# The output projection taken token tile by token tile, and the first up-projection block in token form, in a hybrid decoder layer on one core

## The reference

```python
x = x + (gate_ret * y_ret + gate_moba * y_moba) @ w_out[l]
h = rms_norm(x, ffn_norm[l])
u = causal_depthwise_conv(h @ w_up[l], conv_w[l], conv_b[l])
u_gate, u_val = jnp.split(u, 2, axis=-1)
x = x + (jax.nn.silu(u_gate) * u_val) @ w_down[l]
```

## Time and profile before

| | |
|---|---|
| time, median of 3 runs | 488.93 us (488.80 to 488.98) |
| span of the profiled execution | 486.9 us |
| outside the span (median less span) | 2.0 us |
| PE busy | 475.4 us (98%) |
| PEld busy | 439.7 us (90%) |
| DVE busy | 296.1 us (61%) |
| ACT busy | 249.0 us (51%) |
| POOL busy | 17.1 us (4%) |
| HBM traffic | 177 GB/s over the span |

### The profile page before, as it was taken

How to read it: one execution, slowest core, us unless ns; L and a number is a source line. 1 busy time by engine, 2 the same in 40 slices (tenths; PEclk the granted TensorE clock), 3 DMA queues, 4 the chain that set the end, 5 groups by cost and what they waited for, 6 DMA issues and landing times.

```text
span 486.9 us, 7961 instructions
## 1 busy us (share of the span) xinstructions
PE 475.4 (98%) x3183; PEld 439.7 (90%) x3183; DVE 296.1 (61%) x354; ACT 249.0 (51%) x354; POOL 17.1 (4%) x26
## 2 busy tenths in 40 slices
PE   6999999999999999999999989999999999999997
PEld 4789999888888999999999868999999999988885
DVE  3854884574665546355337856488888777886312
ACT  3735332345884739333444625566666666673310
POOL 1000000311110001000000010000000000000000
PEclk9999999999999999999999997999999999999999
DMA  8996255144455524843453562144545555539002
GB/s 314 355 346 256 104 199 224 48 139 166 168 172 187 219 114 142 333 168 133 165 195 131 194 228 105 69 172 172 176 181 187 194 194 192 189 132 363 3 1 86
DMA packets 13400, 86.65 MB, mean 178 GB/s; under 512 B 1472, under 2 KB 1856, under 8 KB 3648
## 3 DMA queue, kind: packets, MB, share of 16 engines
q1 hardware_dynamic: 12096, 82.84, 45.7%
q10 hardware_dynamic: 864, 1.88, 1.1%
q0 software_dynamic: 416, 1.57, 0.9%
HBM read 85.24 MB, written 1.05 MB: 177 GB/s over the span
## 4 chain that ended last, share of the span: by engine, by line
PE 95%; DMA 1%; DVE 1%; ACT 1%; issue 0%; POOL 0%; POOLq 0%; SPq 0%
PE bank L333 18%; PE bank L334 18%; PE bank L335 18%; PE bank L293 7%; PE bank L295 7%; PE bank L294 7%; PE bank L526 4%; PE bank L523 4%; PE bank L524 4%; PE bank L350 2%; DMA xs<-x_dram 1%; PE bank L429 1%; PE bank L411 1%; PE bank L430 0%; PE bank L410 0%
## 5 line engine op out<-in xcount | busy, mean ns | idle before, releaser
L775 DVE TENSOR_TENSOR w_lo<-w_raw,w_hi 128x2048 fp32r<-128x2048 f32 x75 | 170.3, 2288 | 79.5 <-ACT w_hi L548 79.4
L333 PE MATMUL bank<-h_hi,w_hi 128*128 128x256 f32 x608 | 173.5, 285 | 0.7 <-DVE h_lo L980 0.7
L334 PE MATMUL bank<-h_lo,w_hi 128*128 128x256 f32 x608 | 172.7, 284 | 0.0
L335 PE MATMUL bank<-h_hi,w_lo 128*128 128x256 f32 x608 | 172.7, 284 | 0.0
L548 ACT ACTIVATE w_hi<-w_raw 128x2048 fp32r<-128x2048 f32 x75 | 141.6, 1915 | 33.4 <-PE bank L526 16.9
L333 PEld LDWEIGHTS bank<-h_hi,w_hi 128*128 128x128 f32 x608 | 117.5, 193 | 1.2 <-issue 1.1
L334 PEld LDWEIGHTS bank<-h_lo,w_hi 128*128 128x128 f32 x608 | 117.5, 193 | 0.1
L335 PEld LDWEIGHTS bank<-h_hi,w_lo 128*128 128x128 f32 x608 | 117.4, 193 | 0.0
L293 PE MATMUL bank<-w_hi,h_hi 128*128 128x512 f32 x160 | 63.1, 395 | 0.3 <-DVE w_lo L780 0.2
L295 PE MATMUL bank<-w_hi,h_lo 128*128 128x512 f32 x160 | 62.4, 390 | 0.0
L294 PE MATMUL bank<-w_lo,h_hi 128*128 128x512 f32 x160 | 62.3, 389 | 0.0
(11 more groups left out here) (112 smaller groups left out, 435.4 us busy)
## 6 DMA issues: line engine op xcount, KB each, us to landing
w_raw<-weights_dram SPq DMA_DIRECT2D x76, 1024.0 KB, 4.9
xs<-x_dram SPq DMA_DIRECT2D x2, 512.0 KB, 5.2
w_raw<-weights_dram SPq DMA_DIRECT2D x2, 512.0 KB, 8.3
xs<-x_dram POOLq DMA_DIRECT2D x1, 1024.0 KB, 7.9
out_dram<-ys SPq DMA_DIRECT2D x4, 256.0 KB, 2.0
area<-decay_dram ACTq DMA_DIRECT2D x1, 768.0 KB, 4.1
area<-gain_rows_dram ACTq DMA_DIRECT2D x1, 512.0 KB, 7.0
area<-gain_rows_dram POOLq DMA_DIRECT2D x1, 512.0 KB, 10.7
```

Source lines behind the costliest of these rows:

```text
L333: mm(o, s_hi, r_hi[:, k, :], start=(k == 0 and m % 2 == 0), stop=False)
L334: mm(o, s_hi, r_lo[:, k, :], start=False, stop=False)
L335: ins = mm(o, s_lo, r_hi[:, k, :], start=False, stop=(k == KT - 1 and m % 2 == 1))
L775: tt(w_lo[r][:, :], raw[r][:, :], w_hi[r][:, :].bitcast(f32), ALU.subtract).then_inc(lo_ready, 1)
```

## The change

1. **The output projection goes by token tiles.** For t = 0 all four halves 40 to 43 are taken (12 matmuls each), then for t = 1. Residual, squares, inverse root and normalisation follow for each tile by itself. The transposes of tile 0 stand ahead of the last quarter of tile 1.
2. **The block UP0 (halves 44, 45) is computed in token form**, tile by tile, with the same helper. The transposes of tile 1's normalised activations stand in the middle of tile 0's second half.
3. **It is transposed back.** ACT copies the 128 x 512 result of each token tile to `y_tok` (`up_tok_read`), PE transposes it (4 transposes for a tile: `up_transposes`), the first tile's ahead of the next up block (half 46), the second tile's between halves 46 and 47. ACT copies the transposed tiles to `u_in` and takes the third tap from `u_in` in place of the bank (`up_chan_read`).
4. The first two blocks of the loop are written out, and the loops on PE, ACT and DVE start at 1. The splits of halves 44 and 45 stand behind the squares of tile 0, on ACT and DVE; the splits of 48 and 49 still stand behind the first up block's convolution.

The core of the diff:

```diff
-            for n in range(2 * OUT0, 2 * OUT0 + 4):
-                q = n - 2 * OUT0
-                pe.wait_ge(lo_ready, n + 1)
-                pe.wait_ge(merged_split, 2 if q < 2 else 4)
-                if q < 2:
-                    wait_bank_free(OUT0 + q)
-                tiles = range(4) if q < 2 else range(4, 8)
-                order = [(kk, t) for t in range(NT) for kk in range(4)] if q == 3 else None
-                token_half([block_bank(OUT0 + q % 2, t) for t in range(NT)], n, tiles, q < 2, q >= 2, order,
-                           out_chunk0 if q == 3 else None).then_inc(half_used, 1)
-            for t in range(NT):
+            def one_tile(o, n, t, kh, first, last, after=None):
+                hi = w_hi[n % SLOTS][:, :].rearrange("p (k c) -> p k c", k=4)
+                lo = w_lo[n % SLOTS][:, :].rearrange("p (k c) -> p k c", k=4)
+                for kk in range(4):
+                    k = 4 * kh + kk
+                    s_hi, s_lo = (part[:, k, P * t:P * t + P] for part in (h_hi, h_lo))
+                    mm(o, s_hi, hi[:, kk, :], start=(first and kk == 0), stop=False)
+                    mm(o, s_hi, lo[:, kk, :], start=False, stop=False)
+                    ins = mm(o, s_lo, hi[:, kk, :], start=False, stop=(last and kk == 3))
+                    if after and kk == 1:
+                        after()
+                return ins
+            def h2_transposes(t):
                 for kh in range(2):
                     pe.wait_ge(xn2_ready, 2 * t + kh + 1)
-                    transposes("h2", 2 * t + kh, [y_tok[:, t, P * k:P * k + P] for k in range(4 * kh, 4 * kh + 4)])
+                    transposes(f"h2_t{t}", kh, [y_tok[:, t, P * k:P * k + P] for k in range(4 * kh, 4 * kh + 4)])
+            def up_transposes(t):
+                pe.wait_ge(up_tok_ready, t + 1)
+                transposes("up_chan", t, [y_tok[:, t, P * m:P * m + P] for m in range(4)])
+            for t in range(NT):
+                for q in range(4):
+                    n, kh, c = 2 * OUT0 + q, q // 2, q % 2
+                    if t == 0:
+                        pe.wait_ge(lo_ready, n + 1)
+                        pe.wait_ge(merged_split, 2 * kh + 2)
+                        if kh == 0:
+                            wait_bank_free(OUT0 + c)
+                    ins = one_tile(block_bank(OUT0 + c, t)[:, :], n, t, kh, kh == 0, kh == 1)
+                    if t == 0 and kh == 1:
+                        ins.then_inc(out_summed, 1)
+                    elif t == 1:
+                        ins.then_inc(half_used, 1)
+                    if t == 1 and q == 2:
+                        h2_transposes(0)
+            for t in range(NT):
+                wait_bank_read(pe, OUT0, t)
+                o = block_bank(UP0, t)
+                for h in range(2):
+                    n = 2 * UP0 + h
+                    pe.wait_ge(lo_ready, n + 1)
+                    wait_unit_read(pe, unit(f"h2_t{t}", h))
+                    after = (lambda: h2_transposes(1)) if (t, h) == (0, 1) else None
+                    ins = one_tile(o[:, :], n, t, h, h == 0, h == 1, after)
+                    if t == 0 and h == 1:
+                        ins.then_inc(up_summed, 1)
+                    elif t == 1:
+                        ins.then_inc(half_used, 1)
             def up_half(b, n, free, slot, jj, h):
                 pe.wait_ge(lo_ready, n + 1)
-                for t in range(NT):
-                    wait_unit_read(pe, unit("h2", 2 * t + h))
                 if h == 0:
                     pe.wait_ge(bank_read[jj], free)
                 channel_half([bank[2 * jj], bank[2 * jj + 1]], slot, h_hi, h_lo, h).then_inc(half_used, 1)
-            with pe.Fori(0, UP_BLOCKS // 2) as i:
+            up_transposes(0)
+            for h in range(2):
+                up_half(UP0 + 1, 2 * UP0 + 2 + h, UP0, 2 + h, 1, h)
+                if h == 0:
+                    up_transposes(1)
+            with pe.Fori(1, UP_BLOCKS // 2) as i:
...
+            def up_tok_read(t):
+                if t == 0:
+                    act.wait_ge(up_summed, 1)
+                else:
+                    act.wait_ge(half_used, 2 * UP0 + 2)
+                A(y_tok[:, t, 0:512], block_bank(UP0, t)[:, :], ACT.Copy).then_inc(up_tok_ready, 1)
...
+            for b in range(OUT0):
                 first.get(b, lambda: None)()
-                if b != OUT0:
-                    split(2 * b + 4)
-                    second.get(b, lambda: None)()
-                    split(2 * b + 5)
+                split(2 * b + 4)
+                second.get(b, lambda: None)()
+                split(2 * b + 5)
+            square_x2(0, 0)
+            square_x2(0, 1)
+            split(2 * UP0)
+            split(2 * UP0 + 1)
+            h2_high(0)
+            square_x2(1, 0)
+            square_x2(1, 1)
+            split(2 * UP0 + 2)
+            h2_high(1)
+            up_tok_read(0)
+            split(2 * UP0 + 3)
+            up_tok_read(1)
...
+            def up_chan_read():
+                for t in range(NT):
+                    u = unit("up_chan", t)
+                    act.wait_ge(unit_made, u + 1)
+                    A(u_in[:, 0, :, PAD + P * t:PAD + P * t + P], ubank(u)[:, :].rearrange("p (m s) -> p m s", m=4),
+                      ACT.Copy).then_inc(up_in_ready, 1)
+                act.wait_ge(up_in_ready, NT)
+                for j in range(2):
+                    for m in (2 * j, 2 * j + 1):
+                        c = COL_CONV + 4 * m
+                        ins = A(conv[:, 0, m, :], u_in[:, 0, m, PAD:PAD + SEQ], ACT.Identity,
+                                scale=col[:, c + 2:c + 3], bias=col[:, c + 3:c + 4])
+                    ins.then_inc(bank_read[0], 1)
+                up_silu(0, 1)
             nc.scalar.preload_act_table(ACT.Silu)
-            with act.Fori(0, UP_BLOCKS // 2) as i:
+            up_chan_read()
+            split(2 * UP0 + 4)
+            up_high(0, slice(0, 2), 1)
+            split(2 * UP0 + 5)
+            up_read(1, 2 * UP0 + 4, None, 2, lambda c: col[:, COL_CONV + 16 + c:COL_CONV + 16 + c + 1])
+            split(2 * UP0 + 6)
+            up_high(1, slice(2, 4), 2)
+            split(2 * UP0 + 7)
+            with act.Fori(1, UP_BLOCKS // 2) as i:
...
+            residual(0, 0)
+            residual(0, 1)
+            normalise2(0)
+            split(2 * UP0)
+            split(2 * UP0 + 1)
+            residual(1, 0)
+            h2_low(0)
+            residual(1, 1)
+            normalise2(1)
+            h2_low(1)
+            split(2 * UP0 + 2)
+            split(2 * UP0 + 3)
+            for jj in range(2):
+                nc.vector.memset(u_in[:, jj, :, 0:PAD], 0.0).then_inc(pads_ready, 1)
+            dve.wait_ge(pads_ready, 2)
...
+            for b in range(2):
+                up_conv(b, lambda j: UP0 + j + 1, b + 1,
+                        lambda c: col[:, COL_CONV + 16 * b + c:COL_CONV + 16 * b + c + 1],
+                        lambda s: steps0 + 3 * b + order[s])
+                split(2 * UP0 + 4 + 2 * b)
+                up_low(b, slice(2 * b, 2 * b + 2), b + 1)
+                split(2 * UP0 + 5 + 2 * b)
+            with dve.Fori(1, UP_BLOCKS // 2) as i:
```

More of the change, by code:

```diff
@@ L174, in hybrid_layer @@
         xn2_ready = sem("xn2_ready")
-        h2_hi_ready = [sem(f"h2_hi_ready{kh}") for kh in range(2)]
+        up_summed = sem("up_summed")
+        h2_hi_ready = sem("h2_hi_ready")
+        pads_ready = sem("pads_ready")
+        up_tok_ready = sem("up_tok_ready")
+        up_in_ready = sem("up_in_ready")
         conv_gate_done = sem("conv_gate_done")
@@ L279, in start_unit, with token_half @@
                 return ubank(u)
-            def token_half(out_banks, n, tiles, first, last, order=None, chunk0=None, before=None):
+            def token_half(out_banks, n, tiles, first, last, before=None):
                 hi = w_hi[n % SLOTS][:, :].rearrange("p (k c) -> p k c", k=4)
                 lo = w_lo[n % SLOTS][:, :].rearrange("p (k c) -> p k c", k=4)
-                pairs = order or [(kk, t) for kk in range(4) for t in range(NT)]
-                for kk, t in pairs:
+                for kk, t in [(kk, t) for kk in range(4) for t in range(NT)]:
                     if before and t == 0:
@@ L295, in token_half @@
                     ins = mm(o, s_lo, hi[:, kk, :], start=False, stop=(last and kk == 3))
-                    if chunk0 is not None and (kk, t) == (3, 0):
-                        ins.then_inc(chunk0, 1)
                 return ins
@@ L952, in gate_moba @@
                         .then_inc(merged_split, 1)
-            def residual(b):
-                for t in range(NT):
-                    if b == OUT0:
-                        dve.wait_ge(half_used, 2 * OUT0 + 3)
-                        dve.wait_ge(x_again, 16)
-                    elif t == 0:
-                        dve.wait_ge(out_chunk0, 1)
-                    else:
-                        dve.wait_ge(half_used, 2 * OUT0 + 4)
```

(53 more changed lines are left out.)

53 lines of the change are left out of this document (24 added, 29 removed).

## The result

| | before | changed |
|---|---|---|
| median of 20 runs each | 487.94 us | 489.56 us |
| lowest to highest | 486.56 to 490.20 | 487.87 to 493.53 |
| span of the profiled execution | 486.9 us | 487.5 us |

The changed kernel is slower: ratio 1.004, 95% interval 1.0022 to 1.0059. The forecast was 488.4 us against 488.93, a gain of 0.5 us. The time lies in the range given, the sign is the other one. The 20 runs of the kernel before also show what its first three (488.80 to 488.98) did not: its times fall on levels near 486.7, 488.0, 488.9 and 490.2 us.

A forecast was written before the change was run, and what follows sets the result against it. PE, busy 98%, bounds the kernel. Recovered 6.4 us, less 0.34 for token form and transposing back, 2.45 first wait, 3.1 second wait with starts: 0.5 us gain, 488.93 to 488.4 us; range 487.4 to 490.3.

The forecast's parts named there:

- The first wait: PE, after 24 output projection matmuls, waits for DVE's split of half 42: 2.35 us, plus 0.1 us of slow start.
- The second: PE idle ahead of half 48, whose split stands behind the first up block's convolution: 3.0 to 3.2 us.
- Tile 1's chain: Residual to normalisation of token tile 1, covered by up block tile 0; second normalised half 0.05 us late.
- From the copy to the first tap: ACT's copy of the second transposed token tile to DVE's first tap, on the way to half 48's split.
- from there to the split: DVE's first convolution tap to the split of half 48: 4.48 us, up to 0.15 less in written-out code.
- Half 48 starts: PE begins the loop's half 48 at 319.4 to 319.8, against 320.01 before.
- 6.4 us lost in the hole and to the low clock: PE's loss between output projection and half 48 before the change; all 6.4 us were counted as recovered.
- 0.34 for the block's form and the transposing back: PE work in the first up block: token form saves 0.62 us, transposing back costs 0.96.
- the slow starts: PE's first matmuls behind each of the two new waits: 0.1 us each.
- the first wait is on the safe side: Ahead of half 42: 2.35 us idle with dense work behind it was held not to drop PE's clock.
- the clock falls in the second wait: Rival: PE's clock drops in the wait ahead of half 48, costing 1.5 to 2.9 us, 489.9 to 491.3; chance 0.17.
- HAM oscillation: Skill page section cited for the clock rival: waits between matmul bursts halve PE's clock; by it 489.9 us.

The follow-up runs named there:

- after_again: The changed kernel, unchanged, timed and profiled once more: 489.73 us median, ratio 1.0050 to the kernel before.
- tiles_only: Changed kernel with the first up block back in channel form on the loop, output projection and norm still by token tile: 493.64 us, ratio 1.0112.
- first_wait_covered: Changed kernel with tile 1's first quarter taken between tile 0's second and third quarters, while half 42 is split: 489.28 us median, ratio 1.0011.
- second_wait_covered: Changed kernel with half 48 split ahead of the first up block's convolution, on ACT and DVE: 486.68 us median, ratio 0.9967.
- before_again: The kernel before, unchanged, timed and profiled once more: 486.76 to 490.25 us, ratio 0.9999.

## Why the prediction was wrong

**Right, by its steps.** The first wait: 2.35 us from the end of issue were forecast, 275.91 - 273.35 - 0.227 = 2.33 measured. The second: 3.0 to 3.2, measured 320.50 - 317.36 - 0.12 = 3.02. Tile 1's chain hidden with 0.05 us to spare or to lose: no idle time at 297.38. Timelines of ACT and DVE, answering to the earlier trace rows:

```profile
311.94 0.60 ACT L804 ACTIVATE area<-bank 128x512 f32<-128x512 f32 x1 [4.11 <-PE bank L353]
312.57 2.08 ACT L810 ACTIVATE area<-area,col 128x256 f32<-128x256 f32 x4
...
313.77 3.51 DVE L1107 SCALAR_TENSOR_TENSOR area<-area,col 128x256 f32<-128x256 f32 x8 [9.15 <-ACT area L810]
...
318.07 2.29 DVE L858 TENSOR_TENSOR w_lo<-w_raw,w_hi 128x2048 fp32r<-128x2048 f32 x1
```

From the copy to the first tap 1.83 us (forecast 1.82), from there to the split 4.30 (4.48, with 0.15 named as a possible saving). Half 48 starts 52.4 us behind the output projection's first matmul, as forecast for the full clock (319.4 to 319.8 less 266.97). Against the profiled execution of before the gain is 0.65 us on the way to half 48, forecast 0.4 to 0.5.

**Wrong: the term "6.4 us lost in the hole and to the low clock".** This is the step of the sum that failed. Of it, 2.0 us (slow matmuls and slow transposes) are the low clock, and the trace of one execution was read as if it were in all. In 34 of 58 runs it isn't, by their levels. With the clock full the hole costs 6.4 - 2.0 = 4.4 us, and the same sum reads: 4.4 - 0.34 for the block's form and the transposing back, less 2.33 and 3.02 for the waits with some 0.2 for the slow starts: a loss of 1.5 us, where 1.47 (156.16 - 154.69) is measured. The median of before that the forecast started from, 488.93, came from three runs on one and the same level; 487.94 and 488.28 were the medians of the longer series. Of the 1.6 us between the medians of 20, some 1.2 are the distance of the lowest levels (486.7 and 487.9); the rest fits the low clock being more frequent in the changed kernel, 29 of 32 times against 59 of 83. That the median still fell into the range of 487.4 to 490.3 was partly luck: the upper part of the range was there for a fall of the clock in the second wait, and the fall that the changed kernel's profiles show is in the first.

**Wrong: "the first wait is on the safe side" of the low clock.** That rested on one idle time of 2.28 us in one execution; the changed kernel's profile itself shows the low clock near the start at the same place of the program (granted 0.50 from 12 to 15), and `after_again` shows it behind 2.17 us. The rival "the clock falls in the second wait", with 0.17, was right in its mechanism and its price (1.5 us forecast, 1.4 to 1.6 measured), named only one of the two waits, and its chance was too low. The length of the wait does not decide alone: behind 2.17 us the clock fell in two of four profiled executions, behind 2.85 us in one of three, behind 3.41 us in the only one. The rule from the Trainium skill, "TensorE: Matmul & The Clock Gate", section "HAM oscillation" (waits between bursts of matmuls send the clock back), is borne out only in part in the new waits: by three profiled executions, of `after_again` and `tiles_only` behind the first and of `first_wait_covered` behind the second, and not by the changed kernel's first profile, where the clock is 1.00 behind both, nor by that of `second_wait_covered`.

The gain of the closed hole, then, went to two new waits, which together (5.35 us by the sum above) are longer than the 4.4 us that the hole costs at the full clock. It was not lost to engine work: PE, ACT and DVE are busy for the same time within 2 us.

## What to carry to other kernels

Before a gain is counted, ask whether the loss that it takes away is in every execution: a clock that has fallen in one trace may be full in the next, and then a hole is worth its idle time alone. Take more profiles of the unchanged kernel, or fill its idle times with spare matmuls, and compare at full clock. When PE's order is turned by tiles, every weight half is asked for earlier by the tiles that were put off (24 matmuls instead of 48), and a split that stands behind another block's epilogue keeps its place; both orders must be turned together, and here one moved split was worth 2.8 us, about twice what the change cost.

## What was unexpected of the hardware

The kernel before has four levels of time, 486.7 to 490.2 us, from the same instructions. Near the kernel's start, idle times of PE from 1.2 to 2.4 us (with transposes behind them) are followed by the low clock in some executions and not in others, at 1.2 us; with the idle times filled, six runs lie within 0.4 us. The kernel begins there with 17 extra matmuls. Two executions of before, the first profiled one (clock full there) and `before_again` (granted 0.50 from 11 to 12 us):

```profile
1.45 5.97 PE L362 MATMUL bank<-w_lo 128*128 128x512 f32 x17 [1.45 <-DVE w_lo L800]
9.71 0.63 PE L350 MATMUL bank<-ident,ys 128*128 128x128 f32 x4 [2.28 <-DVE ys L787]
```

```profile
1.45 6.97 PE L362 MATMUL bank<-w_lo 128*128 128x512 f32 x17 [1.45 <-DVE w_lo L800]
9.63 0.63 PE L350 MATMUL bank<-ident,ys 128*128 128x128 f32 x4 [1.21 <-DVE ys L787]
11.01 1.12 PE L350 MATMUL bank<-ident,ys 128*128 128x128 f32 x4 [0.75 <-DVE ys L787]
```

The shorter idle time has the low clock behind it and the longer one has not. Over the 12 profiled executions with 17 extra matmuls the pattern is the same: where these took 5.97 to 6.57 us (six executions, idle for 1.57 to 2.28 us behind them) the clock stayed full, where they took 5.70 to 5.82 or 6.85 to 6.97 us (six, idle for 2.38 to 2.44 or 1.21 to 1.35 us) it fell. So the executions differ from their first microseconds on; why is open. Where in an idle time, or behind how long a one, the clock falls was not measured by itself; shown is only that 2.17 us can be enough and that 1.45, 0.91 and 0.94 us with sixteen transposes between need not be.
